# Feed-forward stage of a two-block transformer kernel: operand sums made one pair earlier, their low halves at a pair's end

## The chip, the cores and the metric

The kernel runs on one core of a Trainium2 chip. The metric is the device time of one execution in microseconds (us). Below, TensorE is PE, VectorE is DVE, ScalarE is ACT and GpSimd is POOL, as in the profile.

## The reference, cut to what matters

Two transformer blocks are computed one after the other, on 256 tokens of width 2048, in float32. Each ends in a gated feed-forward stage of inner width 5632. These stages are what the change touches:

```
hf = rms_norm(x, g_ffn)
x = x + (silu(hf @ w_gate) * (hf @ w_up)) @ w_down        # first block

h2 = rms_norm_2(x, g_ffn_2)
x = x + (silu(h2 @ w_gate_2) * (h2 @ w_up_2)) @ w_down_2  # second block
```

Everything else (attention of three kinds, retention, the last gated embedding) is as it was.

## The kernel before, in words

**Precision.** A float32 product is made of three passes over rounded parts. A weight `w` is split in `w_hi` (ACT copies it to a rounding type, `split` on ACT, L1145) and `w_lo = w - w_hi` (DVE subtracts, `split` on DVE, L1654). Activations are split in the same way (`norm_hi`, `norm_lo` for normed ones, `mix_hi`, `mix_lo` for inner ones). PE then multiplies hi by hi, hi by lo and lo by hi.

**Units.** Weights come in a stream of units of 128x1024 words through rings of four: `raw` (from DRAM), `w_hi` and `w_lo`. A unit costs PE twelve matmuls of 512 columns: eight that need `w_hi`, then four that need `w_lo`. So ACT must make one `w_hi` and DVE one `w_lo` for each unit, and both can be at most four units ahead of PE (`w_used`). Whatever else DVE does stands in one queue with these `w_lo`.

**Pairs.** In the feed-forward stage the inner width is cut in groups of 3, 4 and 4 blocks of 512 columns (`GROUPS`). Block p of group g is the pair `(g, "up", p)`: one gate block and one up block, 16 units in all. After a group's pairs come two pairs `(g, "down", p)` that multiply by `w_down`. I write (0,1) for `(0, "up", 1)`.

**Seven products.** Most pairs (those in `SEVEN`, twelve in each stage; (0,0) and (0,1) are not among them) make four of their 2x2 blocks with seven products instead of eight. That needs sums of the weights, which POOL makes in eight TENSOR_TENSOR instructions per pair (`seven_sums`, L554 to L558), and sums of the activations, which DVE makes once for several pairs:

- `sums_raw` (DVE, L1886 to L1890) adds the hi and lo parts into `tmp_c` (128x1024) and makes four sums S1 to S4 of 128x256 elements. All but the last two are linked: each waits until the one before is done.
- `sums_hi` (ACT, L1251) then makes their hi half, and `sums_lo` (DVE, L1896) the lo half (128x1024).

`sums_raw(False)` and its halves are those of the normed activations: once per stage, in pair (0,1). `sums_raw(True)` is of the inner activations: once for group 0 and once for group 1, both in the pair with p = 2, that is (0,2) and (1,2). The first step of a pair of seven products (`open_seven`, PE L774) is opened by PE inside the pair before it, and waits for `act_ready`, which `sums_lo` raises. The first such opening stands at the end of (0,1).

**The order** of all this is written by hand. The functions `mlp` of ACT and of DVE run through the pairs; in a pair, `steps(n, then)` makes n splits and after the split with number k does what `then[k]` lists. A pair ends like this on DVE: `take_up` (L1709) takes the up block out of PSUM times the gated one, and in the next pair the result `tmp_b` is transposed into `tmp_c` in two groups of eight STREAM_TRANSPOSE (L1789, steps 1 and 2), with one `w_lo` between them.

Of the kernel before, what the change touches and what calls it, by code (L numbers as in the profile page):

```python
# [92 lines left out]
N_SEVEN = len(SEVEN)  # L93
U_MLP = 2 * sum(GROUPS) * (KC // UK) + sum(D // NB * g * CB // UK for g in GROUPS) - 2 * N_SEVEN
# [102 lines left out]
def two_blocks(nc: bass.Bass, stream, seven_in, mem_in, mem_tok, x_in, x_tok, p_in, decay_in, vectors, rows_in,  # L197
               head_rows, consts, tables, positions, out):
    with ExitStack() as ctx:
# [920 lines left out]
        def _(act):  # L1120
# [126 lines left out]
            def sums_hi(hidden):  # L1247

                at = sums_at(hidden)
                act.wait_ge(act_summed, sums_made.add())  # L1250
                act.activation(chunks(heads_r, at), chunks(heads, at + CB), ACT.Copy).then_inc(act_hi_ready, 1)  # L1251
# [11 lines left out]
            def mlp(name, next_name, at, which, final=False, beside=None):  # L1263
# [43 lines left out]
                for g, n in enumerate(GROUPS):  # L1307
                    nd = n * CB // UK
                    for p in range(n):
# [3 lines left out]
                        if (g, p) == (0, 0):  # L1313
                            during(2 * NU - 3, at)
                            wait_rows()
                            gated()
                            split(3)
                            taken.add()
                            continue
                        if j is None:  # L1320
                            sums = {7: [gated], 9: [lambda: sums_hi(False)]}
                            steps(2 * NU, both(early, preparing(after, 5, 6, 8), sums, joining(after, 13)))
                        else:
                            sums = {10: [lambda: sums_hi(True)]} if p == 2 and g < LAST_GROUP else {}
# [307 lines left out]
        def _(dve):  # L1632
# [277 lines left out]
            def mlp(name, next_name, at, which, final=False, beside=None, beside_last=None):  # L1910
# [52 lines left out]
                for g, n in enumerate(GROUPS):  # L1963
                    nd = n * CB // UK
                    for p in range(n):
                        pair = g, "up", p
                        j, after = (seventh(which, q) for q in all_pairs[all_pairs.index(pair):][:2])
                        if (g, p) == (0, 0):
                            during(2 * NU - 3, at)
                            gated(2 * NU - 2)  # L1970
                            split(2)
                            take_up(2)
                            split(1)
                            continue
                        early = {1: [lambda: turning(range(2))], 2: [lambda: turning(range(2, 4), True)],
                                 5: [lambda: hidden_low(p - 1, tmp_c[:, :])]} if p else {}
                        if j is None:
                            sums = {7: [lambda: sums_raw(False, which * N_SEVEN), gated],
                                    10: [lambda: sums_lo(False)], 2 * NU - 1: [take_up]}
                            steps(2 * NU, both(early, preparing(after, 6, 8, 11), joining(after, 13), sums))  # L1980
                        else:
                            sums, used = {}, which * N_SEVEN + (SEVEN.index((g, "up", 2)) if g < LAST_GROUP else 0)
                            if p == 2 and g < LAST_GROUP:
                                sums = {9: [lambda: sums_raw(True, used)], 11: [lambda: sums_lo(True)]}
# [730 lines left out]
```

## Time and profile before

| what | value |
|---|---|
| time, median of 3 runs | 2364.06 us (2363.55 to 2365.42) |
| the profiled execution's own time | 2367.7 us |
| its span, first to last instruction | 2365.9 us |
| PE busy | 2352.9 us, 99% of the span |
| DVE busy | 1948.9 us, 82% |
| ACT busy | 1223.9 us, 52% |
| POOL busy | 403.6 us, 17% |
| mean granted PE clock | 0.998 of full speed |

A busy PE is one that has a matmul in flight. What matters here is the pace: at full clock a 512-column matmul starts every 0.227 us, though each is recorded 0.39 us long. So an idle time of PE in the profile is 0.16 us shorter than the time that the sequence of matmuls lost.

### The profile page before, as it was taken

The page shows a single profiled execution, that of the slowest core. Times are in us where ns is not written, and L with a number is a line of the kernel's source. Part 1 is how long each engine was busy: PE and PEld are TensorE (multiplying, and loading weights), DVE is VectorE, ACT ScalarE, POOL GpSimd, SP SyncE. Part 2 cuts the span into 40 slices and gives each one's busy share as a digit, 9 for nine tenths or more (in the row PEclk, how much of TensorE's full clock was granted, in tenths as well). Part 3 has the DMA queues.
Part 4 walks back from the last instruction along what each step waited for, and adds up shares of the span by engine and source line. Part 5 has one row for each costly group of instructions (what it writes and reads, how often), then busy time and mean ns, then how long its engine had stood idle before and what let it go on. Part 6 is the DMA issues. An engine that isn't in the chain of part 4 may idle for free.

```text
span 2365.9 us, 30942 instructions
## 1 busy us (share of the span) xinstructions
PE 2352.9 (99%) x10692; PEld 1957.8 (83%) x10692; DVE 1948.9 (82%) x2542; ACT 1223.9 (52%) x1639; POOL 403.6 (17%) x290
## 2 busy tenths in 40 slices
PE   9999999999999999999999999999999999999999
PEld 8988888878888788888888888888888888888887
DVE  7788887889888877878897976988988897787885
ACT  6554555645454544545654445455545454464553
POOL 1000000130534335200000000013053433520000
PEclk9999999999999999999999999999999999999999
DMA  8755455656766666665655564566575766665655
GB/s 304 238 176 186 153 170 167 222 196 189 248 203 233 204 228 226 213 213 187 195 196 196 178 196 160 194 239 204 186 251 198 242 213 236 216 214 200 212 190 168
DMA packets 130338, 487.44 MB, mean 206 GB/s; under 512 B 14480, under 2 KB 15120, under 8 KB 129568
## 3 DMA queue, kind: packets, MB, share of 16 engines
q1 hardware_dynamic: 116736, 421.32, 53.6%
q0 software_dynamic: 13184, 64.02, 7.6%
q8 instruction: 86, 1.41, 0.2%
q14 instruction: 44, 0.36, 0.1%
q10 hardware_dynamic: 288, 0.33, 0.0%
HBM read 483.51 MB, written 2.10 MB: 205 GB/s over the span
## 4 chain that ended last, share of the span: by engine, by line
PE 65%; DVE 3%; issue 0%; ACT 0%; ACTq 0%; DVEq 0%
PE acc L627 43%; PE po L627 7%; PE pt L627 6%; PE acc L774 3%; PE pt L774 2%; PE po L774 2%; DVE w_lo L1654 1%; DVE tmp_c L1789 1%; PE acc L664 0%; PE po L965 0%; PE acc L904 0%; PE acc L889 0%; PE po L973 0%; DVE tmp_b L1709 0%; ACT w_hi L1145 0%
## 5 line engine op out<-in xcount | busy, mean ns | idle before, releaser
L1654 DVE TENSOR_TENSOR w_lo<-raw,w_hi 128x1024 fp32r<-128x1024 f32 x796 | 1033.3, 1313 | 299.0 <-ACT w_hi L1145 292.2
L1145 ACT ACTIVATE w_hi<-raw 128x1024 fp32r<-128x1024 f32 x795 | 833.4, 1058 | 797.9 <-PE acc L627 499.2
L627 PE MATMUL acc<-w_hi,norm_hi 128*128 128x512 f32 (+1 forms) x1460 | 568.5, 390 | 0.1
L627 PE MATMUL acc<-w_hi,norm_lo 128*128 128x512 f32 (+1 forms) x1460 | 565.3, 387 | 0.0
L627 PE MATMUL acc<-w_lo,norm_hi 128*128 128x512 f32 (+1 forms) x1460 | 387.5, 387 | 0.0
L627 PE MATMUL acc<-w_hi,mix_hi 128*128 128x512 f32 x832 | 325.1, 391 | 0.8 <-DVE mix_lo L2153 0.8
L627 PE MATMUL acc<-w_hi,mix_lo 128*128 128x512 f32 x832 | 324.0, 389 | 0.0
L627 PEld LDWEIGHTS acc<-w_hi,norm_hi 128*128 128x128 f32 x1460 | 274.2, 188 | 55.8 <-issue 0.8
L627 PEld LDWEIGHTS acc<-w_hi,norm_lo 128*128 128x128 f32 x1460 | 274.2, 188 | 55.1
L627 PEld LDWEIGHTS acc<-w_lo,norm_hi 128*128 128x128 f32 x1460 | 272.9, 188 | 56.0 <-DVE w_lo L1654 0.2
L627 PE MATMUL acc<-w_lo,mix_hi 128*128 128x512 f32 x832 | 222.6, 389 | 0.2 <-DVE w_lo L1654 0.2
L538 POOL DMA_DIRECT2D heads<-seven_in x48 | 26.8, 557 | 968.5 <-PE acc L627 415.2
L627 PEld LDWEIGHTS acc<-w_hi,mix_hi 128*128 128x128 f32 x832 | 156.5, 188 | 33.4 <-ACT w_hi L1452 1.2
L627 PEld LDWEIGHTS acc<-w_lo,mix_hi 128*128 128x128 f32 x832 | 156.0, 188 | 33.3 <-DVE w_lo L1654 1.0
L627 PEld LDWEIGHTS acc<-w_hi,mix_lo 128*128 128x128 f32 x832 | 156.5, 188 | 32.3
L1789 DVE STREAM_TRANSPOSE tmp_c<-tmp_b 32x256 f32<-32x256 f32 x352 | 153.4, 436 | 5.0
L1872 DVE TENSOR_TENSOR heads_r<-heads,heads_r 128x2048 fp32r<-128x2048 f32 (+1 forms) x60 | 126.5, 2108 | 0.0
L554 POOL TENSOR_TENSOR heads<-heads 128x512 f32<-128x512 f32 x48 | 84.1, 1753 | 142.2 <-DMA heads<-seven_in 91.7
L1241 ACT ACTIVATE heads_r<-heads 128x2048 fp32r<-128x2048 f32 x48 | 91.3, 1903 | 7.3 <-POOL tab L558 6.9
L627 PE MATMUL pt<-w_hi,norm_lo 128*128 128x512 f32 x240 | 94.4, 393 | 0.0
L627 PE MATMUL pt<-w_hi,norm_hi 128*128 128x512 f32 x240 | 94.3, 393 | 0.0
L627 PE MATMUL po<-w_hi,norm_hi 128*128 128x512 f32 x240 | 93.4, 389 | 0.0
(354 smaller groups left out, 2934.8 us busy)
## 6 DMA issues: line engine op xcount, KB each, us to landing
raw<-stream SPq DMA_DIRECT2D x795, 512.0 KB, 3.7
heads<-seven_in POOLq DMA_DIRECT2D x48, 768.0 KB, 6.9
heads<-seven_in POOLq DMA_DIRECT2D x12, 512.0 KB, 7.4
tab<-seven_in POOLq DMA_DIRECT2D x12, 512.0 KB, 7.4
heads<-x_in POOLq DMA_DIRECT2D x4, 512.0 KB, 9.0
x<-x_tok POOLq DMA_DIRECT2D x4, 512.0 KB, 7.1
x<-mem_tok POOLq DMA_DIRECT2D x2, 1024.0 KB, 6.6
x<-x_tok POOLq DMA_DIRECT2D x1, 2048.0 KB, 10.1
```

What stands on the lines that cost most here:

```text
L538: pool.dma_start(raw7(step, W11, 3), seven_in[j][:, step * 4 * NB:(step * 4 + 3) * NB])\
L554: after_own(pool.tensor_tensor(raw7(step, T3), raw7(step, T2), raw7(step, T1), ALU.subtract), own + 1)
L627: last = pe.matmul(out_[:, c * NB:c * NB + width], a[:, k * T + c * P:k * T + (c + 1) * P], w[:, s, kk * width:(kk + 1) * width], start=cl ...
L774: last = pe.matmul(bank, a, w, start=clear and i == 0, stop=i == 2, skip_group_check=True)
L1145: act.activation(w_hi[:, (units.fixed - 1) % RING, :], src, ACT.Copy).then_inc(w_hi_ready, 1)
L1241: act.activation(hi7(part, W11, 4), raw7(part, W11, 4), ACT.Copy).then_inc(seven_hi_ready, 1)
L1654: dve.tensor_tensor(w_lo[:, s, :], src, w_hi[:, s, :].bitcast(F32), ALU.subtract)\
L1789: last = dve.transpose(to_rows[:, :, :, of * 32:(of + 1) * 32], rows[of * 32:(of + 1) * 32, :, :, to * 32:(to + 1) * 32])
L1872: dve.tensor_tensor(dst, src, hi.bitcast(F32), ALU.subtract).then_inc(seven_ready, 1)
```

## The change: what it does

It moves three pieces of the sums to other places in the order, in both stages. No instruction is added or removed, and nothing is moved on PE, POOL or the load queue.

1. The sums of the normed activations go from pair (0,1) to the end of (0,0): `sums_raw` behind the splits of `during(2 * NU - 3, at)`, `sums_lo` two splits later, ahead of `take_up`; `sums_hi` on ACT after one split behind the gate.
2. The sums of the inner activations of group 1 go from pair (1,2) to (1,1) (`HIDDEN_SUMS`).
3. Where inner activations are summed, `sums_hi` and `sums_lo` stand at the pair's end, `sums_lo` behind `take_up` and one `w_lo`.

```diff
+HIDDEN_SUMS = ((0, 2), (1, 1))
@@ ACT, mlp
                             during(2 * NU - 3, at)
                             wait_rows()
                             gated()
-                            split(3)
+                            split(1)
+                            sums_hi(False)
+                            split(2)
...
-                            sums = {7: [gated], 9: [lambda: sums_hi(False)]}
-                            steps(2 * NU, both(early, preparing(after, 5, 6, 8), sums, joining(after, 13)))
+                            steps(2 * NU, both(early, preparing(after, 5, 6, 8), {7: [gated]}, joining(after, 13)))
                         else:
-                            sums = {10: [lambda: sums_hi(True)]} if p == 2 and g < LAST_GROUP else {}
+                            sums = {2 * NU - 3: [lambda: sums_hi(True)]} if (g, p) in HIDDEN_SUMS else {}
@@ DVE, mlp
                             during(2 * NU - 3, at)
+                            sums_raw(False, which * N_SEVEN)
                             gated(2 * NU - 2)
                             split(2)
+                            sums_lo(False)
                             take_up(2)
                             split(1)
...
-                            sums = {7: [lambda: sums_raw(False, which * N_SEVEN), gated],
-                                    10: [lambda: sums_lo(False)], 2 * NU - 1: [take_up]}
-                            steps(2 * NU, both(early, preparing(after, 6, 8, 11), joining(after, 13), sums))
+                            ends_ = {7: [gated], 2 * NU - 1: [take_up]}
+                            steps(2 * NU, both(early, preparing(after, 6, 8, 10), joining(after, 13), ends_))
                         else:
-                            sums, used = {}, which * N_SEVEN + (SEVEN.index((g, "up", 2)) if g < LAST_GROUP else 0)
-                            if p == 2 and g < LAST_GROUP:
-                                sums = {9: [lambda: sums_raw(True, used)], 11: [lambda: sums_lo(True)]}
+                            sums, used = {}, which * N_SEVEN + SEVEN.index(pair)
+                            if (g, p) in HIDDEN_SUMS:
+                                sums = {9: [lambda: sums_raw(True, used)], 2 * NU - 2: [lambda: sums_lo(True)]}
```

On DVE, the end of pair (0,0) in the first stage stood so before. The seven `w_lo` end with the last two ahead of `take_up` (L1709); the transposes belong to (0,1).

```order
L1758 SCALAR_TENSOR_TENSOR norm_lo<-tmp_b,vec,norm_hi 128x256 [waits hi_ready]
L1758 SCALAR_TENSOR_TENSOR norm_lo<-tmp_b,vec,norm_hi 128x256 x3
L1654 TENSOR_TENSOR w_lo<-raw,w_hi 128x1024 [waits w_hi_ready] x7
L1709 SCALAR_TENSOR_TENSOR tmp_b<-acc,r_tok,tmp_d 128x512 [waits w_used,block_taken]
L1709 SCALAR_TENSOR_TENSOR tmp_b<-acc,r_tok,tmp_d 128x512
L1654 TENSOR_TENSOR w_lo<-raw,w_hi 128x1024 [waits w_hi_ready,block_taken]
L1654 TENSOR_TENSOR w_lo<-raw,w_hi 128x1024 [waits w_hi_ready]
L1789 STREAM_TRANSPOSE tmp_c<-tmp_b 32x2x4x32 x8
L1654 TENSOR_TENSOR w_lo<-raw,w_hi 128x1024 [waits w_hi_ready]
L1789 STREAM_TRANSPOSE tmp_c<-tmp_b 32x2x4x32 x8
```

It stands so in the changed kernel, whose lines are two higher:

```order
L1656 TENSOR_TENSOR w_lo<-raw,w_hi 128x1024 [waits w_hi_ready] x5
L1888 TENSOR_TENSOR tmp_c<-norm_hi,norm_lo 128x1024 [waits raw_read]
L1889 TENSOR_TENSOR heads<-tmp_c 128x2x128 [waits dve_done]
L1890 TENSOR_TENSOR heads<-heads,tmp_c 128x2x128 [waits dve_done]
L1891 TENSOR_TENSOR heads<-tmp_c 128x2x128 [waits dve_done]
L1892 TENSOR_TENSOR heads<-tmp_c,heads 128x2x128
L1656 TENSOR_TENSOR w_lo<-raw,w_hi 128x1024 [waits w_hi_ready] x2
L1898 TENSOR_TENSOR heads_r<-heads,heads_r 128x1024 [waits act_hi_ready]
L1711 SCALAR_TENSOR_TENSOR tmp_b<-acc,r_tok,tmp_d 128x512 [waits w_used,block_taken]
L1711 SCALAR_TENSOR_TENSOR tmp_b<-acc,r_tok,tmp_d 128x512
L1656 TENSOR_TENSOR w_lo<-raw,w_hi 128x1024 [waits w_hi_ready,block_taken]
L1656 TENSOR_TENSOR w_lo<-raw,w_hi 128x1024 [waits w_hi_ready]
```

Five summing instructions came in ahead of the last two `w_lo` of that stretch, and the lo half ahead of `take_up`; the two groups of transposes follow as before.

The end of pair (1,1) on DVE, before (the first rows are the last `w_lo` ahead of the joining of the seven products, L1903 on; the transposes are those of (1,2)):

```order
L1872 TENSOR_TENSOR heads_r<-heads,heads_r 128x2x512 [waits seven_hi_ready]
L1654 TENSOR_TENSOR w_lo<-raw,w_hi 128x1024 [waits w_hi_ready] x3
L1903 TENSOR_TENSOR tmp_a<-tmp_a,acc 128x512 [waits first_copied]
...
L1654 TENSOR_TENSOR w_lo<-raw,w_hi 128x1024 [waits w_hi_ready] x2
L1709 SCALAR_TENSOR_TENSOR tmp_b<-po,r_tok,tmp_d 128x512 [waits w_used,block_taken]
L1709 SCALAR_TENSOR_TENSOR tmp_b<-po,r_tok,tmp_d 128x512
L1654 TENSOR_TENSOR w_lo<-raw,w_hi 128x1024 [waits w_hi_ready,block_taken]
L1654 TENSOR_TENSOR w_lo<-raw,w_hi 128x1024 [waits w_hi_ready]
L1789 STREAM_TRANSPOSE tmp_c<-tmp_b 32x2x4x32 [waits third_copied]
```

And in the changed kernel:

```order
L1656 TENSOR_TENSOR w_lo<-raw,w_hi 128x1024 [waits w_hi_ready]
L1888 TENSOR_TENSOR tmp_c<-mix_hi,mix_lo 128x1024 [waits third_copied,raw_read,seven_used]
...
L1892 TENSOR_TENSOR heads<-tmp_c,heads 128x2x128
L1656 TENSOR_TENSOR w_lo<-raw,w_hi 128x1024 [waits w_hi_ready] x2
L1905 TENSOR_TENSOR tmp_a<-tmp_a,acc 128x512 [waits first_copied]
...
L1711 SCALAR_TENSOR_TENSOR tmp_b<-po,r_tok,tmp_d 128x512 [waits w_used,block_taken]
L1711 SCALAR_TENSOR_TENSOR tmp_b<-po,r_tok,tmp_d 128x512
L1656 TENSOR_TENSOR w_lo<-raw,w_hi 128x1024 [waits w_hi_ready,block_taken]
L1898 TENSOR_TENSOR heads_r<-heads,heads_r 128x1024 [waits act_hi_ready]
L1656 TENSOR_TENSOR w_lo<-raw,w_hi 128x1024 [waits w_hi_ready]
L1791 STREAM_TRANSPOSE tmp_c<-tmp_b 32x2x4x32 [waits third_copied]
```

The sums came in ahead of the joining, and the lo half between the two `w_lo` that stand ahead of the transposes. The same rows left pair (1,2).

## Rows read from the trace of the kernel before

**Rows 1.** Waits of PE: who, for whom, us in total, times, longest.
```profile
PE pt L774 <- issue: 3.4, 2, 2.4
...
PE pt L627 <- DVE w_lo L1654: 2.3, 2, 1.8
```

**Rows 2.** A window: PE, PEld, DVE, ACT, POOL busy; then PE clock, DMA share, GB/s.
```profile
507.00:516.00 9.00, 6.61 (x23) 4.97 (x22) 6.69 (x6) 1.06 (x1) 0.00 (x0) 0.81 0.69 229
```

**Rows 3.** Timeline of PE, first stage, end of (0,1): start, us, what, [idle before].
```profile
506.93 1.07 PE L627 MATMUL acc<-w_lo,norm_hi 128*128 128x512 f32 x4
510.39 0.47 PE L774 MATMUL pt<-heads_r,norm_hi 128*128 128x512 f32 x1 [2.39 <-issue]
...
515.49 1.32 PE L774 MATMUL po<-heads_r 128*128 128x512 f32 x5
```

**Rows 4.** Timeline of PE, first stage, start of (1,3).
```profile
774.93 0.39 PE L627 MATMUL pt<-w_hi,norm_lo 128*128 128x512 f32 x1
...
780.33 1.20 PE L627 MATMUL pt<-w_lo,norm_hi 128*128 128x512 f32 x4 [1.83 <-DVE w_lo L1654]
...
785.69 0.39 PE L627 MATMUL po<-w_hi,norm_hi 128*128 128x512 f32 x1
```

**Rows 5.** Timeline of PE, the same two places of the second stage.
```profile
1636.51 0.47 PE L774 MATMUL pt<-heads_r,norm_hi 128*128 128x512 f32 x1 [0.99 <-issue]
1903.04 1.21 PE L627 MATMUL pt<-w_lo,norm_hi 128*128 128x512 f32 x4 [0.52 <-DVE w_lo L1654]
```

**Rows 6.** Timeline of DVE, first stage, end of (0,0) and (0,1).
```profile
473.57 4.51 DVE L1654 TENSOR_TENSOR w_lo<-raw,w_hi 128x1024 fp32r<-128x1024 f32 x2 [3.95 <-ACT w_hi L1145]
...
491.21 3.50 DVE L1654 TENSOR_TENSOR w_lo<-raw,w_hi 128x1024 fp32r<-128x1024 f32 x3
...
500.61 1.22 DVE L1886 TENSOR_TENSOR tmp_c<-norm_hi,norm_lo 128x1024 f32<-128x1024 f32 x1
501.86 0.42 DVE L1887 TENSOR_TENSOR heads<-tmp_c 128x256 f32<-128x256 f32 x1
...
509.07 1.22 DVE L1896 TENSOR_TENSOR heads_r<-heads,heads_r 128x1024 fp32r<-128x1024 f32 x1
```

**Rows 7.** Timeline of POOL: one sum of weights by itself, one behind a DVE instruction.
```profile
470.84 1.29 POOL L556 TENSOR_TENSOR heads<-heads 128x512 f32<-128x512 f32 x1
722.28 2.16 POOL L558 TENSOR_TENSOR tab<-tab,heads 128x512 f32<-128x512 f32 x1
```

**Rows 8.** Timeline of PE: when it takes the `w_lo` made at 491.21.
```profile
493.33 1.07 PE L627 MATMUL acc<-w_lo,norm_hi 128*128 128x512 f32 x4
```

**Rows 9.** Timeline of DVE, second stage, end of (0,0), start of (0,1).
```profile
1601.08 4.08 DVE L1654 TENSOR_TENSOR w_lo<-raw,w_hi 128x1024 fp32r<-128x1024 f32 x2 [3.01 <-ACT w_hi L1145]
...
1617.26 3.50 DVE L1654 TENSOR_TENSOR w_lo<-raw,w_hi 128x1024 fp32r<-128x1024 f32 x3
```

**Rows 10.** Timeline of PE: when it takes the `w_lo` made at 1617.26.
```profile
1620.84 0.39 PE L627 MATMUL acc<-w_lo,norm_hi 128*128 128x512 f32 x1
```

**Rows 11.** Timeline of DVE, first stage, end of (1,1), start of (1,2); end of (1,2).
```profile
721.03 4.49 DVE L1654 TENSOR_TENSOR w_lo<-raw,w_hi 128x1024 fp32r<-128x1024 f32 x2
...
734.16 2.36 DVE L1654 TENSOR_TENSOR w_lo<-raw,w_hi 128x1024 fp32r<-128x1024 f32 x2
764.50 1.40 DVE L1709 SCALAR_TENSOR_TENSOR tmp_b<-acc,r_tok,tmp_d 128x512 f32<-128x512 f32 x2
```

**Rows 12.** Timeline of PE: its first matmul behind the up block of (1,2).
```profile
761.10 0.39 PE L774 MATMUL pt<-heads_r,norm_hi 128*128 128x512 f32 x1
```

**Rows 13.** A window at the end of (1,1), first stage, columns as in rows 2.
```profile
706.10:717.30 11.20, 11.20 (x52) 9.26 (x51) 7.19 (x8) 4.10 (x5) 1.82 (x3) 1.00 0.92 299
```

**Rows 14.** Timeline of PE: when it takes the `w_lo` made at 734.16.
```profile
735.65 0.62 PE L627 MATMUL acc<-w_lo,norm_hi 128*128 128x512 f32 x2
```

**Rows 15.** Timeline of DVE, second stage, start of (1,2).
```profile
1857.64 2.36 DVE L1654 TENSOR_TENSOR w_lo<-raw,w_hi 128x1024 fp32r<-128x1024 f32 x2
```

**Rows 16.** Timeline of PE: when it takes the first of these.
```profile
1860.20 0.39 PE L627 MATMUL acc<-w_lo,norm_hi 128*128 128x512 f32 x1
```

## The prediction, as recorded before the run

> **What bounds the kernel now.** I read four views. The page: PE is busy for 2352.9 us of the span, DVE for 82% (the table above). So PE sets the time, all work of other engines is hidden, and only the places where PE stands still are to be had. The change adds no matmul and takes none. Then the waits of PE: two on L774 put down to "issue", 3.4 us in total, and two on `w_lo`, 2.3 us [rows 1]. Then a window around the longest: the granted clock is 0.81 over 9 us [rows 2], which is 1.7 us lost (9 x 0.19; 1.2 instead of 2.4 GHz for 3.4 us). Last the timelines of PE, for what each place costs in all, at 0.227 us a matmul:
>
> - End of (0,1), first stage: the four matmuls that start at 506.93 should be followed at 507.84; the next starts at 510.39, 2.55 late. From there 15 matmuls reach 515.49, 5.10 us instead of 3.40: the half clock. In all 4.25 [rows 3].
> - Start of (1,3), first stage: from 774.93 to 785.69 PE starts 29 matmuls, 6.58 us worth, in 10.76: 4.18. The longest standstill is 1.83 + 0.16 = 1.99; then the half clock [rows 4].
> - The same places of the second stage: 0.99 + 0.16 = 1.15, and with a slow restart 1.25; 0.52 + 0.16 = 0.68, with restart 0.82. The clock stays whole at both [rows 5].
>
> Together 10.5 us, 0.44% of the time. That is all that the change can aim at. What ends the first is a `sums_lo`: it runs 509.07 to 510.28 [rows 6] and PE starts at 510.39 [rows 3]. The second is a `w_lo` behind transposes, on a DVE that had no gap since the sums of (1,2).
>
> **What is removed.** In (0,1) the sums take 1.22 + 4 x 0.42 = 2.9 us from 500.61 on and the lo half another 1.1 of DVE's queue (an instruction of 1.22 starts 1.13 before the next one), 4.0 us in all [rows 6]. With the sums made in (0,0), PE's opening needs only the weights' halves, and those stand in the queue ahead of where the sums_lo stood. I take both stalls of L774 as gone: -4.25 and -1.25. In (1,2) the same 4.0 us leave. `take_up` there ran at 764.50 [rows 11] though PE had gone on from its block at 761.10 [rows 12], so up to 3.4 us of the 4.0 come through to the transposes and the `w_lo` behind them, more than the 2.0 by which that was late [rows 4]. -4.18 and -0.82. The halves of group 0's inner sums, moved behind `take_up` in (0,2), are neither more nor less for a queue that is full on both sides; the nearest `w_lo` has as much to spare as before. I cost this at nothing; without that cover it would be one instruction, 1.13.
>
> **What is added, (0,0), first stage.** Before, DVE was idle for 3.95 us up to 473.57, that is from 469.62 [rows 6]. This gap looks like the room for the sums. From 473.57 to the `w_lo` at 491.21 it had no gap: 17.64 us. Three of the `w_lo` in it took 1.1 longer than 1.22 (two of them are 4.51 together), since POOL was at its sums of weights: 14.4 of DVE's own work. POOL does one such sum in 1.29 by itself, and takes 2.16 when a DVE instruction is in front [rows 7]; so they go one at a time, each waiting for the other's, about 1.1 us a wait.
>
> From 469.62 on POOL has seven sums before it. The moved work is five instructions and one more, and each of them, and each `w_lo`, gives POOL its turn. If every one waits, all seven POOL sums stand in DVE's way: 469.62 + 14.4 + 4.0 + 7 x 1.1 = 495.7, when the `w_lo` behind the second transposes starts, instead of 491.21. It ends 1.2 later, 496.9. PE wants it at 493.33 [rows 8]: **3.6 us lost**, of which some 2.2 in one piece and the rest at three `w_lo` before it.
>
> The trace shows this wait for 128x1024 only. The four small sums (0.42 each) never stood beside POOL. Bounds: if the small ones don't wait, POOL does two or three of its sums beside them and `take_up`, and about five waits of 1.1 are left: the `w_lo` ends at 494.7, 1.4 lost. I take 3.6, since they are the same instruction with the same two inputs in SBUF as those that wait. The Trainium skill, page "SBUF — State Buffer", section "Who interferes with whom", says that a DVE instruction with two SBUF inputs contends with a GpSimd instruction that reads SBUF, and that the one that comes second blocks fully. It names no size; by it the sum is 3.6, without it 1.4. It speaks against this change, for the gap of 3.95 is then no room for six instructions.
>
> **(0,0), second stage.** DVE is idle from 1598.07 to 1601.08; then 16.18 to the `w_lo` at 1617.26, with 1.7 of waits in it: 14.5 of work [rows 9]. POOL is further along, five sums are left. And ACT, which makes the sums' hi half only when they are done, then makes the next `w_hi` 0.9 later than DVE could use it. 1598.07 + 14.5 + 4.0 + 5 x 1.1 + 0.9 = 1623.0; it ends 1624.2, and PE wants it at 1620.84 [rows 10]: **3.3 lost**, 2.2 of it in one piece. If the small ones don't wait, 1.3.
>
> **(1,1).** The sums themselves (2.9) fall where DVE is busy for 7.19 of 11.2 us, 4.0 free, and POOL only issues its loads (1.82) [rows 13]: nothing. Without that room it would be 2.9 more. The lo half goes between the `w_lo` of 721.03 and the next. From there to 734.16 DVE has no gap [rows 11] and POOL is at work (722.28 is in it [rows 7]): 1.1 of its own and one more wait of 1.1, 2.2. The `w_lo` at 734.16 ended 0.27 before PE took it at 735.65 [rows 14]. **1.9 lost**, in one piece. In the second stage the same `w_lo` ends at 1858.87 and is taken at 1860.20, 1.33 to spare [rows 15, 16]: **0.9 lost**. Bounds: 0.9 and 0 if POOL happens to be silent.
>
> **The sum.** Gained 10.5; lost 3.6 + 3.3 + 1.9 + 0.9 = 9.7: -0.8 us. Then the clock. A standstill of 1.99 was followed by the half clock, one of 1.15 was not [rows 4, 5]. The two new ones of 2.2 are beyond the first, so I count 1.7 for each; that of 1.9 lies between, nearer to 1.99, yet under all that were shown to bring it, and I leave it out. -0.8 + 3.4 = +2.6. The profiled execution is 2367.7 with a span of 2365.9 and the median of the runs 2364.06; the difference is worked within one trace and set on the median: **2366.7 us**. A change of under 0.2% (4.7 us) is about what a measurement of this kernel can't tell from none.
>
> **Rivals.**
>
> - *The small sums don't wait for POOL.* For it: no row shows a small one waiting. Lost is then 1.4 + 1.3 + 1.9 + 0.9 = 5.5, no standstill above 1.9, no half clock: 10.5 - 5.5 = 5.0 gained, 2359.1 us, faster by 0.21%. It needs also that 1.9 keeps the clock. 0.20 for faster, with the case that POOL is luckier placed.
> - *Each wait costs a whole POOL sum.* For it: a sum alone is 1.29, not 1.1. The 14 waits above then cost 0.19 more each, +2.7, all three long standstills pass 1.99 and bring 5.1 of half clock: -0.8 + 2.7 + 5.1 = +7.0, 2371.1 us, slower, 0.15 of the 0.20. It decides from 0.4 us more loss on, once the third half clock (which alone makes +4.3) is there. Against it: the two waits in the 4.51 are 1.1 each [rows 6].
> - *The place in (1,2) stays late,* since what left it is eaten up by waits for PE there: then only 2 of the 5.0 come back, +5.6 in all, 2369.7, slower by 0.24%. Against it: `take_up` stood 3 us behind its block. Its chance is 0.05, in the 0.20 for slower.
>
> **How the numbers follow.** Forecast, no change that can be told (-0.8 with no half clock to +4.3 with three): 0.60. Faster 0.20, slower 0.20. The range reaches from the first rival, 2359.0, to near the second, 2370.5.
>
> **What the profile after would show.** No wait on L774 at the end of (0,1), in either stage; no wait at 778. The first of the sums in (0,0) beside POOL recorded at about 2.2 instead of 1.22, and the small ones at about 1.5 instead of 0.42: if these read 0.42, the forecast is wrong at that step. New waits of PE on `w_lo` near 495 (2.2), near 737 (1.9), 1622 (2.2) and 1861 (0.9), and the granted clock under 1 behind the first and third. A prediction well off would come from the clock (half clocks that stay out or come at 1.9) or from POOL starting its sums at another moment, since its loads land within a microsecond or so of a fixed point.

## The result, and the profile after

The changed kernel takes 2370.32 us (median of 8 executions, 2366.19 to 2373.57), the kernel before beside it 2363.81 (2361.93 to 2365.42): a ratio of 1.0025, with a 95% interval of 1.0016 to 1.0034. It is slower, by 0.25%, just over what a measurement can tell. The forecast was 2366.7 and "no change that can be told"; the time lies inside the range, 0.2 us below its upper end (2370.5). The profiled execution took 2373.57 us, the longest of the eight, with a span of 2371.8.

The waits of PE, as in [rows 1]:

```profile
PE acc L628 <- DVE w_lo L1656: 8.7, 7, 1.9
PE acc L628 <- DVE mix_lo L2156: 1.9, 1, 1.9
PE pt L775 <- DVE po L1909: 1.3, 2, 0.7
```

Both waits for "issue" on the opening step are gone, and so is the wait at the start of (1,3). In their place PE waits seven times for a `w_lo`. The second line stands at the start of the program, at 8.8 us, far ahead of the change. The third is new: a join of the seven products in the pair (0, "down", 1).

Where these waits stand, in the timeline of PE (start, us, what, [idle before]); the first two rows show how a loss is read off: from 496.55 to 498.81 are 2.26 us where a matmul's pace is 0.227, so 2.03 are lost.

```profile
496.55 0.39 PE L628 MATMUL acc<-w_hi,norm_lo 128*128 128x512 f32 x1
498.81 1.20 PE L628 MATMUL acc<-w_lo,norm_hi 128*128 128x512 f32 x4 [1.87 <-DVE w_lo L1656]
...
605.46 0.47 PE L775 MATMUL pt<-heads_r,mix_hi 128*128 128x512 f32 x1 [0.64 <-DVE po L1909]
...
740.88 1.20 PE L628 MATMUL acc<-w_lo,norm_hi 128*128 128x512 f32 x4 [1.86 <-DVE w_lo L1656]
...
1624.80 1.21 PE L628 MATMUL acc<-w_lo,norm_hi 128*128 128x512 f32 x4 [1.87 <-DVE w_lo L1656]
...
1866.94 1.20 PE L628 MATMUL acc<-w_lo,norm_hi 128*128 128x512 f32 x4 [1.87 <-DVE w_lo L1656]
```

What a place costs in all is the time from a matmul ahead of it to one behind it, less 0.2267 us for each matmul between them (the pace over a stretch of 50 us without a stop); the shorter stops and the slow restarts are in it. So counted, the places lose: (0,0) and the start of (0,1) 3.4 us in the first stage and 3.2 in the second; the start of (1,2) 3.2 and 3.1; (0, "down", 1) 0.9 and 0.9. In all 14.7, against 10.7 that are gone (the prediction's 10.5, and restarts at (1,3) of the second stage that it left out). With the 2.3 us that the start of the program lost more, this is the 5.9 us by which the span grew, to within 0.3. The windows behind the long stops (PE, PEld, DVE, ACT and POOL busy; clock; DMA share; GB/s) and the one at the start:

```profile
494.00:503.00 9.00, 7.13 (x30) 5.58 (x31) 8.71 (x13) 5.46 (x5) 0.00 (x0) 1.00 0.50 153
...
736.00:745.00 9.00, 7.14 (x30) 5.58 (x31) 7.39 (x12) 5.40 (x5) 0.00 (x0) 1.00 0.44 136
...
5.00:14.00 9.00, 7.12 (x24) 5.27 (x23) 5.76 (x7) 6.01 (x10) 1.22 (x2) 0.81 0.97 337
```

The granted clock stayed whole behind all four stops of 2.0 us, where the forecast had counted two half clocks. One came at the start of the program instead, behind a stop for the first loads. The start lost 2.3 us more here than in the trace before. No instruction there has changed, and between all fourteen traces of this case the start differs by up to 3.4 us, so I take it as chance. It is not shown: the second trace of the changed kernel is high there too.

DVE in (0,0), with the first of POOL's eight adds (the sums of weights), to be read against [rows 6] and [rows 7]:

```profile
464.80 4.62 DVE L1656 TENSOR_TENSOR w_lo<-raw,w_hi 128x1024 fp32r<-128x1024 f32 x4
466.82 3.76 POOL L555 TENSOR_TENSOR heads<-heads 128x512 f32<-128x512 f32 x1 [25.21 <-PE acc L628]
...
471.90 2.19 DVE L1888 TENSOR_TENSOR tmp_c<-norm_hi,norm_lo 128x1024 f32<-128x1024 f32 x1
474.13 1.40 DVE L1889 TENSOR_TENSOR heads<-tmp_c 128x256 f32<-128x256 f32 x1
...
478.31 1.50 DVE L1892 TENSOR_TENSOR heads<-tmp_c,heads 128x256 f32<-128x256 f32 x1
479.74 4.56 DVE L1656 TENSOR_TENSOR w_lo<-raw,w_hi 128x1024 fp32r<-128x1024 f32 x2
484.23 1.21 DVE L1898 TENSOR_TENSOR heads_r<-heads,heads_r 128x1024 fp32r<-128x1024 f32 x1
```

The forecast's test is passed: the small sums read 1.40 to 1.50 instead of 0.42. Here a DVE instruction of two SBUF inputs costs 1.0 to 1.1 us more beside a POOL add, at 128x256 as at 128x1024. The first add is the exception: it took 3.76 us itself, and the four `w_lo` beside it kept their pace (4.62 for four). By the Trainium skill (page "SBUF — State Buffer", section "Who interferes with whom") such an instruction contends with GpSimd's reads; the trace agrees, with 1.40 for 0.42. Only the lo half was spared, since POOL had ended at 483.2.

In (1,1) the loss came in another way than forecast. ACT, DVE, and the queues in 712:724 (KB each, median us to landing):

```profile
719.79 1.04 ACT L1252 ACTIVATE heads_r<-heads 128x1024 fp32r<-128x1024 f32 x1
723.87 1.06 ACT L1146 ACTIVATE w_hi<-raw 128x1024 fp32r<-128x1024 f32 x1 [3.04 <-DMA raw<-stream]
```
```profile
725.03 1.70 DVE L1656 TENSOR_TENSOR w_lo<-raw,w_hi 128x1024 fp32r<-128x1024 f32 x1 [1.94 <-ACT w_hi L1146]
726.66 2.32 DVE L1898 TENSOR_TENSOR heads_r<-heads,heads_r 128x1024 fp32r<-128x1024 f32 x1
```
```profile
raw<-stream SPq DMA_DIRECT2D x4, 512.0 KB, 7.9
heads<-seven_in POOLq DMA_DIRECT2D x2, 768.0 KB, 7.1
```

The sums at step 9 delay the two `w_lo` behind them, and a `w_lo` is what frees a slot of `raw`. The next load of weights was so issued at 714.92, just behind POOL's three loads (713.59 to 714.84, 2 MB together), and took 8.9 us to land where the median load of weights takes 3.7 (the 7.9 of the row is the median of the four loads in that window). It landed at 723.8. ACT waited 3.04 us for it and DVE stood idle for 1.94 in a pair whose DVE queue had nothing to spare.

### The profile page after: what moved, and what is told of

The parts are those of the page before. It is cut to its first block and busy times, and to the rows that moved or that the text cites. A ratio compares the mean times of both kernels' runs of the same rounds, so it can differ in the third digit from the quotient of the medians.

```text
span 2371.8 us, 30942 instructions
## 1 busy us (share of the span) xinstructions
PE 2353.3 (99%) x10692; PEld 1956.8 (83%) x10692; DVE 1951.9 (82%) x2542; ACT 1223.8 (52%) x1639; POOL 399.5 (17%) x290
## 5 line engine op out<-in xcount | busy, mean ns | idle before, releaser
L628 PE MATMUL po<-w_hi,norm_lo 128*128 128x512 f32 x240 | 93.5, 390 | 0.0
```

Of the source, the lines that this page charges most:

```text
L628: last = pe.matmul(out_[:, c * NB:c * NB + width], a[:, k * T + c * P:k * T + (c + 1) * P], w[:, s, kk * width:(kk + 1) * width], start=cl ...
```

## The experiments

A ratio is against the kernel before, timed beside each version. A loss is counted over a whole place as above.

### The kernel before, once more

No edit. 

> The kernel before, unchanged, for a second trace. Theory A (what left the four old places is small in a usual execution): the trace shows standstills of about 2.5 and 1.2 us at the ends of (0,1) and 2.2 and 0.8 at the start of (1,3), but no half clock behind them, so the four cost about 7 us, not 10.5, and the execution is some 3 us under the 2367.7 of the first trace. Rival B (the changed kernel pays in half clocks): the two half clocks are here again, the four places cost 10.5 us. Ratio to the kernel before: 1.000 within 0.001.

Measured: 2365.49 us, ratio 1.0005 (0.9996 to 1.0014). The profiled execution has a span of 2361.7, 4.2 us less than the first one. PE's waits, and the window at the start of (1,3):

```profile
PE pt L774 <- issue: 3.4, 2, 2.4
PE pt L627 <- DVE w_lo L1654: 1.6, 1, 1.6
```
```profile
774.00:790.00 16.00, 16.00 (x72) 13.26 (x71) 14.45 (x13) 12.56 (x12) 0.00 (x0) 1.00 0.52 169
```

The stop at the end of (0,1) is there again (4.3 with its half clock, and 1.3 in the second stage). The 4.18 of (1,3) [rows 4] are not: 72 matmuls in 16 us, no time lost, while the second stage lost 2.1 there instead of 1.0. What the change could remove was 7.6 us in this execution, not 10.7. That is near theory A's sum, though not for its reason: one half clock stayed, and a whole stop was missing.

### The normed sums alone

Part 1 of the change, on ACT and on DVE (with `preparing` from step 11 to 10 in (0,1), as in the change); the rest as before.

```diff
@@ DVE, mlp
                             during(2 * NU - 3, at)
+                            sums_raw(False, which * N_SEVEN)
                             gated(2 * NU - 2)
                             split(2)
+                            sums_lo(False)
                             take_up(2)
```


> Only the sums of the normed activations are moved, from (0,1) to (0,0). Theory A: lost at the w_lo of (0,0) and (0,1) 3.1 + 2.9 us, as in the trace of the changed kernel, gained 2.5 + 1.2 (without half clock): slower by 1.5 to 3 us, ratio 1.0006 to 1.0013. Rival B: 5.5 gained with the half clock and up to 3.4 of half clocks lost: between 0.5 and 4 us slower, with the granted clock at half near 500 or 1624 in the trace. Small sums beside POOL read 1.40 us, not 0.42.

Measured: 2367.75 us, ratio 1.0018 (1.0009 to 1.0027). It loses 3.4 us at (0,0) in the first stage and 3.2 in the second, the same as the whole change. The two stops at (1,3), which this version keeps, cost 1.0 each: a third value from the same place. The ratio is above theory A's range. A had put the stops that go at 3.7; in this way of counting they cost 5.5 in the two traces of before. No half clock came with the new stops, so rival B is not borne out either, though the time lies at the edge of its range.

### The inner sums and their halves alone

Parts 2 and 3 of the change; (0,0) and (0,1) as before.

```diff
-                            if p == 2 and g < LAST_GROUP:
-                                sums = {9: [lambda: sums_raw(True, used)], 11: [lambda: sums_lo(True)]}
+                            if (g, p) in HIDDEN_SUMS:
+                                sums = {9: [lambda: sums_raw(True, used)], 2 * NU - 2: [lambda: sums_lo(True)]}
```


> Only the sums of the inner activations are moved: group 1 a pair sooner, halves at the pair's end. Theory A: lost at the transposes of (1,2) 2.9 us in each stage, gained 2.2 + 0.8, and up to 0.9 lost in each stage at (0,down,1), where POOL's first sum now comes ahead of a w_lo: slower by 3 to 4.5 us, ratio 1.0012 to 1.0019. Rival B: gained 4.2 + 0.8 with the half clock: slower by 1 to 2.5 us. If the 0.9 of (0,down,1) comes from the moved halves of (0,2), it is here and not in the kernel with the normed sums alone.

Measured: 2366.94 us, ratio 1.0013 (1.0004 to 1.0022), in theory A's range. Timeline of PE at the end of (0,1), and windows behind two stops:

```profile
511.86 0.47 PE L775 MATMUL pt<-heads_r,norm_hi 128*128 128x512 f32 x1 [2.40 <-issue]
...
1861.02 1.40 PE L628 MATMUL acc<-w_lo,norm_hi 128*128 128x512 f32 x4 [1.87 <-DVE w_lo L1655]
```
```profile
507.00:516.00 9.00, 6.60 (x29) 5.16 (x28) 8.16 (x7) 2.06 (x3) 0.00 (x0) 1.00 0.67 217
...
1857.00:1866.00 9.00, 7.13 (x25) 5.42 (x24) 7.41 (x11) 6.25 (x5) 0.00 (x0) 0.81 0.54 173
```

The same 2.56 us stop that brought the half clock in two traces of before kept the full clock here, and a stop of 2.03 us at (1,2) brought it. So the length of the stop alone does not decide it; what does, no run here shows. At (0, "down", 1) no more than 0.1 us was lost in either stage, though the halves of (0,2) are moved here. Each of the two parts is slower than before, and their ratios add up (1.0018 and 1.0013) to the whole's 1.0025 within the intervals.

### The changed kernel, once more

No edit. 

> The changed kernel, unchanged, for a second trace and more runs. Theory A: ratio 1.0020 to 1.0032 (some 5 to 7.5 us), the sum of the two parts; standstills of 2.03 us near 497, 740, 1623 and 1866 with a whole clock behind them. Rival B: a half clock behind at least two of them. The 2.0 us wait at the very start (for the first loads) is chance and not in each execution.

Measured: 2372.43 us, ratio 1.0037 (1.0023 to 1.005). The window behind the stop in (0,1), to be read against the same window above:

```profile
494.00:503.00 9.00, 7.12 (x25) 5.40 (x24) 8.72 (x13) 6.24 (x5) 0.00 (x0) 0.81 0.57 176
```

Same kernel, same stop (2.04 us), now with the half clock: 5.0 us lost in (0,0) and (0,1). The start of (1,2) lost only 1.4 in either stage, where the other trace had 3.2 and 3.1. There the load of weights was issued 0.55 us behind the first of POOL's loads, instead of 1.33, and landed in 6.1 us instead of 8.9. (0, "down", 1) lost 1.0 in the first stage and nothing in the second. The ratio is above theory A's range, and one half clock in the feed-forward stages is one too many for A and too few for B. The start lost 1.5 us more than in the first trace before, with a half clock there as well.

### POOL's adds sooner

```diff
-                    pool.wait_ge(w_used, U_MLP_AT[0] + 12)
+                    pool.wait_ge(w_used, U_MLP_AT[0] + 11)
...
-                    pool.wait_ge(w_used, U_MLP_AT[1] + 12)
+                    pool.wait_ge(w_used, U_MLP_AT[1] + 9)
```


> The changed kernel, with POOL's first sums of the seven products let go one unit sooner in the first feed-forward stage and three units sooner in the second; nothing else differs. The port theory (the moved sums are dear only because POOL's adds of 128x512 run beside them, 1.4 us a small sum against 0.42 and 2.2 to 2.3 us a large one against 1.2): TensorE's loss in pair (0,0) falls from 3.2 us to 1.5 or less in the first stage and from 2.9 to under 1 in the second, and the time falls by some 3.5 us from that of the changed kernel, to about 2367. The rival (the length of VectorE's queue itself, whatever POOL does, since five sums and a half stand ahead of a low half there): both losses stay at 2.5 us or more and the time stays within 1 us of the changed kernel's.

Measured: 2369.57 us, ratio 1.002 (1.0011 to 1.0029); the first stage lost 4.4 us at (0,0), the second 1.3. The theory fell in the first stage; in the second the loss fell by more than half, though not under 1. The time stayed within 1 us of the changed kernel's, as the rival had it. DVE there:

```profile
463.42 11.24 DVE L1656 TENSOR_TENSOR w_lo<-raw,w_hi 128x1024 fp32r<-128x1024 f32 x5
474.70 2.20 DVE L1888 TENSOR_TENSOR tmp_c<-norm_hi,norm_lo 128x1024 f32<-128x1024 f32 x1
476.93 1.39 DVE L1889 TENSOR_TENSOR heads<-tmp_c 128x256 f32<-128x256 f32 x1
478.36 0.42 DVE L1890 TENSOR_TENSOR heads<-heads,tmp_c 128x256 f32<-128x256 f32 x1
```

Three small sums are back at 0.42, but five `w_lo` ahead of them now take 2.25 each. That is what I had overlooked: POOL has eight adds, and while DVE has work, an add is paid by one DVE instruction, about 1 us, whichever it is. In the changed kernel seven instructions of this stretch paid 7.2 us together (0.96 + 3 x 0.98 + 1.08 + 2 x 1.1), and the first add was paid by POOL. Here eight paid 8.5: the four `norm_lo` ahead of these rows, 2.71 us instead of 1.67, met the first add, then five `w_lo` and two sums the others. That is one more than in the changed kernel, and the stage lost 1.0 us more. In the kernel before DVE was idle through half of POOL's adds, and three paid 3.2 [rows 6]. Moving POOL gains only where it lands on idle time of DVE, as in the second stage.

### The inner sums of (1,1) later, halves right behind

```diff
-  sums = {2 * NU - 3: [lambda: sums_hi(True)]} ...                       # ACT
+  sums = {10 if g == 0 else 11: [lambda: sums_hi(True)]} ...
...
-  sums = {9: [lambda: sums_raw(True, used)], 2 * NU - 2: [lambda: sums_lo(True)]}   # DVE
+  sums = {9 if g == 0 else 11: [lambda: sums_raw(True, used)],
+          11 if g == 0 else 12: [lambda: sums_lo(True)]}
```


> The changed kernel, with the halves of (0,2) back at their old steps, and in (1,1) the five sums at step 11 and both halves right behind them, ahead of the take-up, instead of sums at step 9 and the low half at the end. The theory that the sums at step 9 free a weight slot too late, so that its next load queues behind POOL's four loads: the time in which VectorE stands for a high half at some 723 us goes from 1.9 us to under 0.5, TensorE's loss at the start of (1,2) falls from some 2 to 3 us to under 1 in either stage, and the 0.9 at (0,down,1) may go or stay; the time falls by 2 to 5 us from the changed kernel's, to 2366 to 2369. The rival (any five sums and halves in (1,1) cost TensorE their own 5 us less the idle time that was there, wherever they stand): the loss stays at 2 us and the time within 1 us of the changed kernel's.

The halves of (0,2) are back at their old steps. Measured: 2365.57 us, ratio 1.0005 (0.9996 to 1.0014), 4.8 under the changed kernel and 0.4 under the range. PE's waits for `w_lo`, and ACT's first wait for a load there:

```profile
PE acc L628 <- DVE w_lo L1656: 4.1, 4, 1.9
```
```profile
723.38 1.06 ACT L1146 ACTIVATE w_hi<-raw 128x1024 fp32r<-128x1024 f32 x1 [0.41 <-DMA raw<-stream]
```

Nothing is lost at the start of (1,2), in either stage; the four waits left are those of (0,0). ACT's wait for the load is 0.41 instead of 3.04: the load that came behind POOL's was issued at 710.66 here, ahead of them (711.22), and landed in 5.7 us. So 2.9 us of sums and 1.2 of a half do fit into (1,1); step 9 and the end were the wrong places. Which of the two moves gained how much, this version does not show, since it makes both.

### POOL sooner and the inner sums later, together

> Both edits, POOL's earlier start and the later sums of (1,1) with the halves at their old steps in (0,2). If the two causes are separate, the gains add: some 2362 us, 6 to 9 below the changed kernel and 1 to 3 below the one before, with a loss left of about 1.5 us in (0,0) of the first stage. If they are one (VectorE's whole queue is too long for these pairs), no more than the better of the two is seen.

Measured: 2364.67 us, ratio 1.0002 (0.9993 to 1.0011). The window over the whole of (1,1) and (1,2)'s start:

```profile
700.00:760.00 60.00, 60.00 (x267) 49.67 (x266) 52.69 (x60) 31.10 (x33) 17.21 (x14) 1.00 0.68 232
```

PE never stops there. The time is 5.7 us under the changed kernel's, not 6 to 9, since POOL sooner gave nothing in the first stage (4.4 lost). That the two gains add is in keeping with this, but the 0.8 of POOL sooner alone is not clear of noise.

### The inner sums alone, placed so

The kernel before, with the inner sums of group 1 in (1,1) and at the later steps.

```diff
-                            if p == 2 and g < LAST_GROUP:
-                                sums = {9: [lambda: sums_raw(True, used)], 11: [lambda: sums_lo(True)]}
+                            if (g, p) in HIDDEN_SUMS:
+                                sums = {9 if g == 0 else 11: [lambda: sums_raw(True, used)],
+                                        11 if g == 0 else 12: [lambda: sums_lo(True)]}
```


> The kernel before with only the inner sums of the second group moved, from (1,2) to (1,1), at step 11 with both halves right behind them; the sums of the normed activations stay in (0,1). Against the kernel before it takes away the wait at the start of (1,3) (4.2 and 0.8 us in the first trace, none and 1.9 in the second) and adds nothing if the placement is what was wrong: 1 to 4 us below before, about 2361.5. If the sums in (1,1) cost TensorE their time wherever they stand, it is at or above before, 2364 to 2367, as the version with sums at step 9 and halves at the end was (2366.9).

Measured: 2363.29 us, ratio 0.9992 (0.9983 to 1.0001). By the ratio this is 1.9 us under the kernel before, in the range of the expectation but not clear of none. (1,2) and (1,3) lost 0.9 in all. But PE lost 0.9 and 1.1 us at (0, "down", 1), and here group 0's halves stood at their old steps. So part 3 of the change is not what makes that stop. Timelines of DVE and POOL there, in this version:

```profile
599.38 2.11 DVE L1655 TENSOR_TENSOR w_lo<-raw,w_hi 128x1024 fp32r<-128x1024 f32 x1
```
```profile
599.11 1.29 POOL L556 TENSOR_TENSOR heads<-heads 128x512 f32<-128x512 f32 x1
```

The same two engines in the kernel before, with no stop:

```profile
599.26 1.22 DVE L1654 TENSOR_TENSOR w_lo<-raw,w_hi 128x1024 fp32r<-128x1024 f32 x1
```
```profile
599.49 2.15 POOL L554 TENSOR_TENSOR heads<-heads 128x512 f32<-128x512 f32 x1 [4.84 <-DMA heads<-seven_in]
```

The last `w_lo` ahead of the join takes 1.22 when POOL's first add, which starts when its load lands, comes 0.2 us behind it, and 2.1 when POOL is already adding (here its second add began 0.3 us ahead). The order of the two is decided by a fraction of a microsecond in that landing: of the fourteen traces some show it in one stage, some in both, some in none.

### The normed sums one unit sooner

```diff
-                            during(2 * NU - 3, at)
+                            during(2 * NU - 4, at)
                             sums_raw(False, which * N_SEVEN)
+                            split(1)
```


> The changed kernel, with the five sums of (0,0) issued one unit sooner, ahead of VectorE's low half of unit u152 instead of behind it; nothing else differs. In the trace of the changed kernel VectorE was idle for 1.2 us ahead of that unit, and POOL began its adds at 473.1, 1.2 us behind the first sum. Theory (every VectorE operation that runs while POOL adds waits for one POOL add, about 1 us more whichever it is, and POOL's eight adds are worth seven or eight of these; operations moved to where POOL is idle and VectorE waits for a high half are free): the five sums take 2.9 us instead of 7.9, the first stage's loss at (0,0) and (0,1) falls from 3.2 us to 0.3 to 1.5, the second's (where POOL begins earlier) stays near 2.9, and the time falls by 1.5 to 3 us from the changed kernel's. Rival (VectorE's work of these pairs is simply more than TensorE's time for them): the first stage's loss stays above 2.5 us.

Measured: 2369.69 us, ratio 1.0024 (1.0015 to 1.0034): nothing gained that can be told; (0,0) lost 3.2 in the first stage, as before this edit, and 1.9 instead of 3.2 in the second. The expectation rests on a misreading of mine: POOL had not begun at 473.1 but at 466.8 (its third add stands at 473.1). DVE and POOL in this version:

```profile
466.85 2.20 DVE L1888 TENSOR_TENSOR tmp_c<-norm_hi,norm_lo 128x1024 f32<-128x1024 f32 x1
469.09 1.40 DVE L1889 TENSOR_TENSOR heads<-tmp_c 128x256 f32<-128x256 f32 x1
```
```profile
464.22 3.75 POOL L555 TENSOR_TENSOR heads<-heads 128x512 f32<-128x512 f32 x1 [25.20 <-PE acc L628]
```

In the first stage all five sums still met POOL's adds, so the idea was not tested there.

### All pieces in idle places, and POOL later

Both versions have the later inner sums. In (0,0) the five sums stand two units sooner than in the changed kernel, the hi half right behind them and the lo half two `w_lo` later, both ahead of the gate. The second version also lets POOL's adds go three units later in the second stage.

```diff
-                            during(2 * NU - 3, at)
+                            during(2 * NU - 5, at)
                             sums_raw(False, which * N_SEVEN)
+                            split(2)
+                            sums_lo(False)
                             gated(2 * NU - 2)
...
-                    pool.wait_ge(w_used, U_MLP_AT[1] + 12)     # second version only
+                    pool.wait_ge(w_used, U_MLP_AT[1] + 15)
```


> All three moved pieces put where VectorE is idle: the five sums of (0,0) two units sooner than in the changed kernel, both halves right behind, ahead of the gate; the sums of (1,1) at step 11 with their halves behind them; the halves of (0,2) at their old steps. Theory: the first stage loses nothing at (0,0) and (0,1) (slack of the last low half before the second turning 0.5 us or more, as in the kernel before), nothing at (1,2), up to 0.9 at (0,down,1) by chance; in the second stage, where POOL begins three units earlier and meets all five sums, 0 to 1.5 us are left at (0,0). The time is 3 to 6 us below the kernel before: 2358 to 2361. Rival (whole queue too long): 2364 to 2366, as the version with the later sums of (1,1) alone.

> The same with POOL's adds of the second stage let go three units later, as late against the units as in the first stage, so that the sums and halves there are over before POOL begins. Theory: the loss at (0,0) of the second stage goes as well; the time is as before or up to 1.5 us less. Rival (POOL's later end makes ScalarE's and VectorE's halves of the seven products' weights late): a new wait on a low half of those at the start of (0,1), and the time is 1 us or more higher.

Measured: 2361.72 us, ratio 0.9994 (0.9985 to 1.0003), and 2360.96, ratio 0.9988 (0.9979 to 0.9997). The first misses its range by 0.7 us, since the theory was wrong on the first stage: POOL begins at 463.5, the sums at 465.0, so they met it still. Both versions stopped PE there, at a `w_lo` behind sums that took 7.9 us; the place lost 3.2 and, with a half clock, 3.8. In its second stage the first version lost 1.5 us.

```profile
475.15 1.60 PE L628 MATMUL acc<-w_lo,norm_hi 128*128 128x512 f32 x4 [1.79 <-DVE w_lo L1655]
```

That row is of the version with POOL later. In its second stage the sums stood in DVE's idle time beside an idle POOL, and no time was lost there:

```profile
1586.38 1.23 DVE L1887 TENSOR_TENSOR tmp_c<-norm_hi,norm_lo 128x1024 f32<-128x1024 f32 x1
1587.64 0.43 DVE L1888 TENSOR_TENSOR heads<-tmp_c 128x256 f32<-128x256 f32 x1
```

### POOL later in both stages

```diff
-                    pool.wait_ge(w_used, U_MLP_AT[0] + 12)
+                    pool.wait_ge(w_used, U_MLP_AT[0] + 15)
```


> The version with all pieces in idle places and POOL's adds let go three units later in the second stage, now with the same three units in the first stage as well: POOL begins at about 471.6 instead of 463.5, and the five sums of (0,0) (465.0 to 472.8 in the version before this one, 1.4 to 1.5 us a small one) are over before it begins. Theory (a VectorE operation beside a POOL add costs about 1 us more, whichever it is; beside an idle POOL nothing): the sums take 2.9 us and the low half 1.2, the last low half ahead of TensorE's standstill at 473.0 to 476.6 comes in time, its 2.6 us and the half clock behind it are gone, and the time falls by 1.5 to 4 us more, to 2357 to 2359.5. Rival (POOL's end, 8 us later, meets VectorE's take-up and transposes of (0,1), and the slack of 0.9 us there is used up): 1 to 3 us are lost at the second turning of (0,1) instead and the time is 2360 to 2362.

Measured: 2357.44 us (2356.34 to 2359.45), ratio 0.9973 (0.9964 to 0.9982). This version beats both kernels clearly: it is 6.4 us under the one before, 13 under the changed one. The theory held, the rival fell. PE's waits in the feed-forward stages for DVE, DVE in (0,0), and POOL's first add:

```profile
PE pt L775 <- DVE po L1908: 0.6, 2, 0.4
PE acc L628 <- DVE w_lo L1655: 0.5, 1, 0.5
```
```profile
465.44 1.23 DVE L1887 TENSOR_TENSOR tmp_c<-norm_hi,norm_lo 128x1024 f32<-128x1024 f32 x1
466.70 0.42 DVE L1888 TENSOR_TENSOR heads<-tmp_c 128x256 f32<-128x256 f32 x1
...
473.04 3.69 DVE L1655 TENSOR_TENSOR w_lo<-raw,w_hi 128x1024 fp32r<-128x1024 f32 x2 [1.25 <-ACT w_hi L1146]
```
```profile
472.12 1.29 POOL L555 TENSOR_TENSOR heads<-heads 128x512 f32<-128x512 f32 x1 [33.37 <-PE acc L628]
```

The sums and the half are over before POOL begins, and DVE even waits for ACT behind them. (0,0) and (0,1) lose nothing in either stage. The places of this case now lose 2.1 us (0.9 at (1,2), 0.4 and 0.7 at (0, "down", 1)).

## Why the prediction was right, and where it was off

The forecast was no change that can be told, and the ratio lies just above that line (its interval begins at 1.0016); the time is 3.6 us over the forecast. It is inside the range by 0.2 us only, and the second measurement of the same kernel, 2372.43, lies above it. That it fell inside the range is luck as much as foresight. The new waits stand where they were looked for: near 495, 1622 (2.0 instead of 2.2), 737 (1.9 forecast, 2.0 at 741) and 1861 (0.9 forecast, 2.0 at 1867). By its steps:

**Removed, 10.5 us: the mechanism right, the size too large.** All four stops went. But the trace that they were read from was itself 3.6 us over the kernel's median, and I set the difference on the median. The executions in which a place was unchanged give, for the start of (1,3), both stages together, 5.2, 2.1 and 2.0 us; for the end of (0,1) 4.3, 4.3, 4.3 and 2.7, and 1.3 each in the second stage. The means are 3.1 and 5.2: 8.2 us (8.23) in place of 10.5. Of the 3.6 us over the forecast this term explains 2.3.

**Added in (0,0), 3.6 and 3.3: right.** Four traces have this placement: 3.3 to 3.4 in the first stage and 3.1 to 3.2 in the second, half clocks (two, of 1.7) apart. The small sums did wait, so the first rival fell; a wait cost 0.96 to 1.1, so the second fell too. What the runs add is where the cost comes from: it follows the number of POOL's adds that run while DVE has work, not the kind of instruction that they meet. With POOL's adds later, the same six instructions in (0,0) cost PE nothing.

**Added in (1,1), 1.9 and 0.9: too small.** Five traces have this placement (the version with the inner sums alone, and the two with POOL's adds or the normed sums sooner are among them): 3.2 and 3.1, 1.4 and 1.4, 2.2 and 4.6 (with a half clock), 2.2 and 2.1, 3.2 and 2.0, a mean of 5.1 for both stages against 2.8. The failed step is "4.0 free, and POOL only issues its loads: nothing". I counted DVE's time and not what a late `w_lo` holds up, a slot of `raw` and with it the load behind POOL's. Where that load took 8.2 to 8.9 us to land, the place lost 2.2 to 3.2 (half clock apart); in the four cases in which it took 6.0 or 6.1, it lost 1.4 to 2.1. So about 1 us of each loss goes with the late load, and the rest is there without it, which is what the lo half with its wait was forecast to cost, or somewhat more. In the later placement the same instructions cost nothing.

**(0, "down", 1), costed at nothing: 0.9 and 0.9, 1.0 and 0.** Not by the moved halves alone: the inner sums alone have them and lost nothing there, and a version without them lost 0.9 and 1.1. It hangs on whether POOL's load lands ahead of a `w_lo` or behind it; whether the change made the bad case likelier, these traces are too few to say.

**Two half clocks, +3.4: wrong as a rule.** In the feed-forward stages of the fourteen traces, stops of 1.86 to 2.04 us were followed by the half clock 5 times in 20, stops of 2.55 or 2.56 us 3 times in 4. The changed kernel had none there in one trace and one in the other. By these counts, which nobody had then, the term should have been about a quarter of 1.7 for each such stop. It made good, by chance, a part of what the other terms lacked.

With the measured means, half clocks as they came: 7.3 in (0,0) + 5.1 in (1,1) + 1.2 in (0, "down", 1) (the four traces in which both sets of sums are moved as in the change) = 13.6 added, 8.2 removed, +5.4. The two ratios are +5.9 (3.8 to 8.0) and +8.7 us (5.4 to 11.8). Up to three microseconds stay open. The start of the program may be a part of them: in the two traces of the changed kernel it lost 1.5 to 3.4 us more than in the two of before, while two versions with the same instructions there (POOL's adds sooner, the normed sums one unit sooner) stayed below the first trace of before. The third rival, that (1,3) stays late, fell: it lost nothing there in any trace with the sums moved.

## What to carry to other kernels

Take what a change can remove from several executions, not from one: here a stop of one trace cost 4.2 us and was missing in the next. When work is moved into an engine's idle time, ask what runs then on the engine that it contends with, and move one of the two; the same instructions cost PE 3 us where DVE met a working POOL and nothing where POOL was idle. And a queue with idle time is not free if what it frees, a buffer slot, starts a load: look at which loads stand just behind.

## What the runs showed of the hardware

A DVE instruction of 128x256 elements with two SBUF inputs takes 1.40 us instead of 0.42 beside a POOL add of 128x512, one of 128x1024 2.2 to 2.3 instead of 1.22: about the same 1.0 to 1.1 us at a quarter of the size, as a wait would give and a slower rate would not. POOL can be the one that pays: its first add took 3.76 us while four `w_lo` ran at their usual pace. PE's half clock is no sure thing behind a stop of one length: it came after 5 of 20 stops near 2 us and stayed out after one of four of 2.56. A load of 512 KB issued just behind 2 MB of other loads took 8.9 us to land, against 3.7 for the median load of that size from the same queue; issued 0.55 us behind the first of them, in the second trace, it took 6.1.
